# Regrouping the matmuls of a contraction step: pass by pass over the PSUM banks instead of chunk by chunk

## The chip, the core and the metric

The kernel runs on one NeuronCore of a Trainium2 chip. The metric is the device time of one execution in microseconds (us); for the kernel before it is 3276.52 us, the median of 3 runs.

## The reference, cut to what matters

One inference step of a two-layer decoder trunk of width 2048 over 1024 prompt positions and 8 x 8 sample positions, which makes 1088 token columns. All weights and activations are fp32.

```
layer 0:  z = rms_norm(h) @ w_in_a            # 2048 x 6144: a, b, gate
          c = a * sigmoid(b); y = silu(layer_norm(causal depthwise conv31(c)))
          h = h + rms_norm((y * silu(gate)) @ w_out_a)          # 2048 x 2048
layer 1:  k, v = rms_norm(h) @ w_kv           # 2048 x 512, 4 kv heads
          q, gate = rms_norm(h) @ w_in_b      # 2048 x 4096, 32 heads of 64
          o = sliding-window attention (128) with a sink per head
          h = h + rms_norm((o * silu(gate)) @ w_out_b)          # 2048 x 2048
```

Nearly all of the arithmetic is in the products with the weights, and they are what the change touches.

## The kernel before, in words

The data lie feature-major: 128 features on the partitions, 16 blocks of features (KT), 1088 tokens along the free axis. An output tile is 128 output features by all tokens. Its sum runs over 16 steps k, one for each block of input features. The products are made to near fp32 accuracy in three passes of a cheaper matmul type: activations and weights are each split into a rounded part (u_hi, w_hi) and the rest (u_lo, w_lo), and a tile sums u_hi\*w_hi, u_lo\*w_hi and u_hi\*w_lo.

The 1088 tokens are cut into three chunks of 364, 364 and 360 columns (CHUNKS). Each chunk of a tile has a PSUM bank of its own: z_even and z_odd are three banks each, and tiles alternate between the two. The PE function `tile(n, z, ...)` issues one tile. Its argument cs says which chunks take part: ALL (three chunks, 9 matmuls a step, 144 a tile), HEAD (the two chunks of 364 columns, 6 a step, 96 a tile) or TAIL (the chunk of 360 alone, 3 a step, 48 a tile). The program has 100 ALL tiles (32 for a and b of layer 0, called the GLU stage here, 16 for its gate, 16 for its output, 4 for k and v, 32 for q and the gate of layer 1), then 16 HEAD tiles and 16 TAIL tiles for the last output projection. Every matmul is preceded by a load of its 128x128 weights into the array, also when the weights are those of the matmul before it.

Inside a step the order before is: for each chunk the u_hi matmul (line 515) and then the u_lo matmul (line 516), both with w_hi and both into the same bank; after that, for each chunk, the w_lo matmul (line 518). So the w_lo pass already goes from bank to bank, while the other two passes write each bank twice in a row.

Around the matmuls, engines follow one another by semaphores, and each engine's order is written out by hand. The DMA queue of SP brings the weights in quarters of a tile (4 steps) to w_raw; ScalarE rounds them to w_hi (line 744) once PE has used the quarter of the tile before (w_used, raised by the last w_lo matmul of the quarter); GpSimd makes w_lo = w_raw - w_hi (line 1030) and raises w_lo_ready, for which PE waits ahead of each quarter. VectorE and ScalarE read a finished tile's three banks (z_read), and PE waits for that before it writes the same three banks two tiles later. In the GLU stage VectorE also computes the depthwise convolution (line 1327). In the q and gate tiles of layer 1 the attention matmuls are put between the steps of every second tile by the callback after_k.

Of the kernel before, what the change touches and what calls it, by code (L numbers as in the profile page):

```python
# [35 lines left out]
P = 128  # L36
# [6 lines left out]
CHUNKS = [(0, 364), (364, 364), (728, 360)]  # L43
# [46 lines left out]
def trunk_kernel(nc, x_t, state_t, ck_t, cv, w, cols_in, y_t, scp_t, ckp_t, cvp, scs_t, cks_t, cvs):  # L90
    ctx = ExitStack()
    with ctx:
        def sb(name, shape, dt=F32):
            return ctx.enter_context(nc.sbuf_tensor(name, shape, dt))
# [13 lines left out]
        u_hi = sb("u_hi", [P, KT, T], F32R)  # L108
        u_lo = sb("u_lo", [P, KT, T], F32R)
        w_raw = sb("w_raw", [P, NQ, 512])  # L110
        w_hi = sb("w_hi", [P, NQ, 512], F32R)
# [29 lines left out]
        cs = cs_flat.rearrange("p (b s) -> p b s", b=SB)  # L141
# [136 lines left out]
        def ge(eng, s, v):  # L278

            if not (isinstance(v, int) and v <= 0):  # L280
                eng.wait_ge(s, v)
# [4 lines left out]
        def chunk(ap, c):  # L286
            return ap[:, CHUNKS[c][0]:CHUNKS[c][0] + CHUNKS[c][1]]
# [213 lines left out]
        def _(pe):  # L501
            def tile(n, z, before_k=None, after_k=None, order=range(KT), cs=ALL):

                ge(pe, z_read, n - 1)
                seen = [0] * NQ
                for i, k in enumerate(order):
                    if before_k is not None:
                        before_k(i)
                    q, at = k // 4, P * (k % 4)
                    if seen[q] == 0:  # L510
                        pe.wait_ge(w_lo_ready, NQ * n + q + 1)
                    seen[q] += 1
                    for c in cs:
                        o = z[:, c, 0:CHUNKS[c][1]]
                        pe.matmul(o, w_hi[:, q, at:at + P], chunk(u_hi[:, k, :], c), start=(i == 0), stop=False)  # L515
                        pe.matmul(o, w_hi[:, q, at:at + P], chunk(u_lo[:, k, :], c), start=False, stop=False)  # L516
                    for c in cs:
                        mm = pe.matmul(z[:, c, 0:CHUNKS[c][1]], w_lo[:, q, at:at + P], chunk(u_hi[:, k, :], c),  # L518
                                       start=False, stop=(i == KT - 1))
                    if seen[q] == 4:  # L520
                        mm.then_inc(w_used, 1)
                    if after_k is not None:
                        after_k(i)
# [23 lines left out]

            pe.transpose(aux[:, 0, 0:SS], causal_ts[0:SS, :], ident[0:SS, 0:SS]).then_inc(mask_turned, 1)
            tile(0, z_even, lambda k: pe.wait_ge(u_lo_ready, k + 1))
            pe.wait_ge(sq_added, KT - 1)  # L550
            for c in range(3):
                mm = pe.matmul(z_odd[:, c, 0:CHUNKS[c][1]], ones[:, :], chunk(r_a, c), start=True, stop=True)
            mm.then_inc(sq_summed, 1)
            pe.wait_ge(var_ready, 1)
            tile(1, z_odd)
            with pe.Fori(1, KT) as i:
                tile(2 * i, z_even)
                tile(2 * i + 1, z_odd)
# [1045 lines left out]
```

## Time and profile before

| | us |
|---|---|
| median of 3 runs | 3276.52 (3274.56 to 3279.51) |
| the profiled execution | 3278.45 |
| its span | 3276.8 |
| PE busy in the span | 3075.6 (94%) |
| weight loads busy in the span | 2962.2 (90%) |
| VectorE, GpSimd, ScalarE busy | 1506.5, 1548.1, 850.2 |
| mean granted TensorE clock | 0.974 |
| matmuls, and weight loads | 19117 each |

The span is the profile's time from the first to the last instruction; the profiled execution's own time lies 1.65 us above it. A matmul's length in the records (0.33 us) is about twice the time from one start to the next, because matmuls are pipelined; what a matmul costs in a dense stretch is the distance of starts, and it is read from the timeline.

### The profile page before, as it was taken

The numbers are of one execution on the slowest core, as the hardware profiler recorded it, in microseconds if no ns is written. First come the engines' busy times: TensorE is split into PE (matmuls) and PEld (weight loads), VectorE is DVE, ScalarE is ACT, GpSimd is POOL, SyncE is SP. The second block draws the span as 40 slices with busy tenths as digits, with TensorE's granted clock in tenths as the row PEclk, the third lists the DMA queues.
The fourth block names the chain that finished last, engine by engine and source line by source line (L and its number), as shares of the span: only waits on it lengthen the run. The fifth ranks groups of instructions, "written<-read, shape, count | busy, mean of one in ns | idle before, by whom it ended". The sixth has DMA issues, their size and how long they took to land.

```text
span 3276.8 us, 50429 instructions
## 1 busy us (share of the span) xinstructions
PE 3075.6 (94%) x19117; PEld 2962.2 (90%) x19117; DVE 1506.5 (46%) x1729; ACT 850.2 (26%) x1708; POOL 1548.1 (47%) x1153
## 2 busy tenths in 40 slices
PE   6999999999989999999968999999999999899996
PEld 6999999999989999999947899899899889799985
DVE  6999999999931114000082233433443443500043
ACT  5121112211122214122142222322322322422332
POOL 2778778787733333333344233333333323244475
PEclk9999999999999999999989999999999999899998
DMA  5121221212122224222273211211211211432386
GB/s 163 41 71 50 57 60 47 71 50 57 51 92 95 89 96 170 71 65 72 86 253 113 64 48 43 61 45 45 58 42 48 61 39 48 157 95 87 108 290 219
DMA packets 171676, 284.86 MB, mean 87 GB/s; under 512 B 62008, under 2 KB 72504, under 8 KB 171576
## 3 DMA queue, kind: packets, MB, share of 16 engines
q1 hardware_dynamic: 127328, 222.48, 22.2%
q10 hardware_dynamic: 41912, 52.32, 4.4%
q0 software_dynamic: 2352, 8.88, 0.7%
q8 instruction: 60, 0.98, 0.1%
q14 instruction: 24, 0.20, 0.0%
HBM read 218.44 MB, written 67.15 MB: 87 GB/s over the span
## 4 chain that ended last, share of the span: by engine, by line
PE 46%; issue 23%; DVE 16%; ACT 5%; POOL 5%; DMA 3%; ACTq 1%; DVEq 1%; SPq 0%; POOLq 0%
PE z_even L515 8%; PE z_even L516 8%; PE z_even L518 8%; PE z_odd L515 7%; PE z_odd L516 6%; PE z_odd L518 6%; POOL w_lo L1030 3%; DVE aux L1327 3%; DVE work L1327 2%; DMA work<-conv_scratch 2%; ACT work L948 1%; DVE work L1423 1%; POOL work L1139 1%; DVE work L1426 1%; DVE work L1429 1%
## 5 line engine op out<-in xcount | busy, mean ns | idle before, releaser
L1030 POOL TENSOR_TENSOR w_lo<-w_raw,w_hi 128x512 fp32r<-128x512 f32 x528 | 745.2, 1420 | 1364.7 <-ACT w_hi L744 1364.2
L515 PE MATMUL z_even<-u_hi,w_hi 128*128 128x364 f32 (+1 forms) x2784 | 926.8, 333 | 88.9 <-POOL u_lo L1191 33.8
L515 PE MATMUL z_odd<-u_hi,w_hi 128*128 128x364 f32 (+1 forms) x2784 | 939.3, 337 | 58.0 <-POOL w_lo L1030 58.0
L516 PE MATMUL z_even<-u_lo,w_hi 128*128 128x364 f32 (+1 forms) x2784 | 923.0, 332 | 0.0
L516 PE MATMUL z_odd<-u_lo,w_hi 128*128 128x364 f32 (+1 forms) x2784 | 922.8, 331 | 0.0
L744 ACT ACTIVATE w_hi<-w_raw 128x512 fp32r<-128x512 f32 x528 | 331.3, 630 | 1681.7 <-PE z_even L518 804.6
L518 PE MATMUL z_odd<-u_hi,w_lo 128*128 128x364 f32 (+1 forms) x2784 | 636.6, 330 | 0.0
L518 PE MATMUL z_even<-u_hi,w_lo 128*128 128x364 f32 (+1 forms) x2784 | 635.9, 330 | 0.0
L515 PEld LDWEIGHTS z_even<-u_hi,w_hi 128*128 128x128 f32 x2784 | 531.0, 191 | 106.9 <-issue 35.8
L515 PEld LDWEIGHTS z_odd<-u_hi,w_hi 128*128 128x128 f32 x2784 | 531.6, 191 | 96.7 <-POOL w_lo L1030 54.5
L516 PEld LDWEIGHTS z_odd<-u_lo,w_hi 128*128 128x128 f32 x2784 | 532.2, 191 | 0.1
L516 PEld LDWEIGHTS z_even<-u_lo,w_hi 128*128 128x128 f32 x2784 | 531.7, 191 | 0.4 <-issue 0.3
L518 PEld LDWEIGHTS z_odd<-u_hi,w_lo 128*128 128x128 f32 x2784 | 488.4, 190 | 0.0
L518 PEld LDWEIGHTS z_even<-u_hi,w_lo 128*128 128x128 f32 x2784 | 487.7, 190 | 0.0
L1327 DVE SCALAR_TENSOR_TENSOR work<-work,cols 128x1024 f32<-128x1024 f32 x224 | 422.1, 1884 | 0.0
L1327 DVE SCALAR_TENSOR_TENSOR aux<-work,cols,aux 128x1024 f32<-128x1024 f32 x240 | 306.4, 1277 | 38.7 <-ACT aux L788 38.5
L1268 DVE TENSOR_SCALAR work<-z_even 128x364 f32<-128x364 f32 (+1 forms) x6 | 2.9, 530 | 657.4 <-PE z_even L543 657.4
L1278 DVE TENSOR_TENSOR work<-z_even,work 128x364 f32<-128x364 f32 (+1 forms) x126 | 59.4, 525 | 506.2 <-PE z_even L518 506.2
L1111 POOL TENSOR_TENSOR work<-work 128x480 f32<-128x480 f32 (+3 forms) x128 | 152.4, 1191 | 10.0
L1022 POOL TENSOR_TENSOR w_raw<-w_raw,cols 128x512 f32<-128x512 f32 x144 | 148.3, 1040 | 18.6 <-DMA branch_scratch<-work 18.6
L1103 POOL TENSOR_TENSOR work<-work,cols 128x248 f32<-128x248 f32 x128 | 130.2, 1048 | 2.9 <-POOL work L1115 2.9
L1139 POOL TENSOR_TENSOR work<-work 128x1088 f32<-128x1088 f32 x16 | 42.5, 2657 | 152.8 <-ACT work L809 140.1
(149 smaller groups left out, 2174.4 us busy)
## 6 DMA issues: line engine op xcount, KB each, us to landing
w_raw<-in_w SPq DMA_DIRECT2D x528, 256.0 KB, 2.6
work<-in_x SPq DMA_DIRECT2D x32, 544.0 KB, 5.3
work<-branch_scratch SPq DMA_DIRECT2D x31, 544.0 KB, 5.4
conv_scratch<-work ACTq DMA_DIRECT2D x16, 544.0 KB, 2.7
work<-conv_scratch SPq DMA_DIRECT2D x16, 544.0 KB, 3.8
resid_scratch<-work ACTq DMA_DIRECT2D x16, 544.0 KB, 5.6
branch_scratch<-work ACTq DMA_DIRECT2D x16, 512.0 KB, 2.6
branch_scratch<-work POOLq DMA_DIRECT2D x15, 544.0 KB, 3.0
```

The costliest lines, as they stand in the source:

```text
L515: pe.matmul(o, w_hi[:, q, at:at + P], chunk(u_hi[:, k, :], c), start=(i == 0), stop=False)
L516: pe.matmul(o, w_hi[:, q, at:at + P], chunk(u_lo[:, k, :], c), start=False, stop=False)
L518: mm = pe.matmul(z[:, c, 0:CHUNKS[c][1]], w_lo[:, q, at:at + P], chunk(u_hi[:, k, :], c), start=False, stop=(i == KT - 1))
L744: act.activation(w_hi[:, q, :], w_raw[:, q, :], ACT.Copy).then_inc(w_hi_ready, 1)
L948: ins = act.activation(sc[u][:, i, :], sc[u][:, i, :], ACT.Exp, scale=HD ** -0.5, bias=st[:, 4 + i:5 + i], accum_out=st[:, 16 + i:17 + i])
L1022: pool.tensor_tensor(w_raw[:, q, :].rearrange("p (k c) -> p k c", k=4), w_raw[:, q, :].rearrange("p (k c) -> p k c", k=4), cols[:, gain + ...
L1030: pool.tensor_tensor(w_lo[:, q, :], w_raw[:, q, :], w_hi[:, q, :].bitcast(F32), ALU.subtract).then_inc(w_lo_ready, 1)
L1103: ins = pool.tensor_tensor(pr[:, b], win, cols[:, bass.ds(C_CW + j * CW, CW)].unsqueeze(1).to_broadcast([P, SS, CW]), ALU.mult)
L1111: pool.tensor_tensor(pm[:, :, 0:m], pm[:, :, 0:m], pm[:, :, other:other + m], ALU.add).then_inc(pool_step, 1)
L1139: pool.tensor_tensor(s_st0, yb0[par], gg0[par], ALU.mult).then_inc(s_ready, 1)
L1278: ins = dve.tensor_tensor(chunk(out, c), z[:, c, 0:CHUNKS[c][1]], chunk(by, c), ALU.mult)
L1327: dve.scalar_tensor_tensor(out=acc, in0=cp[:, i:i + TP], scalar=cols[:, bass.ds(C_CW + j * CW + i, 1)], in1=acc, op0=ALU.mult, op1=ALU.add ...
```

## The change

In a step, the u_hi matmuls now go over all chunks first, then the u_lo matmuls go over all chunks, then the w_lo matmuls as before. No instruction is added or taken away, and the sum that each bank collects has the same terms. For a TAIL tile, with one chunk, the order is the one it had.

```diff
--- before.py
+++ after.py
@@ -511,9 +511,11 @@
                         pe.wait_ge(w_lo_ready, NQ * n + q + 1)
                     seen[q] += 1
                     for c in cs:
-                        o = z[:, c, 0:CHUNKS[c][1]]
-                        pe.matmul(o, w_hi[:, q, at:at + P], chunk(u_hi[:, k, :], c), start=(i == 0), stop=False)
-                        pe.matmul(o, w_hi[:, q, at:at + P], chunk(u_lo[:, k, :], c), start=False, stop=False)
+                        pe.matmul(z[:, c, 0:CHUNKS[c][1]], w_hi[:, q, at:at + P], chunk(u_hi[:, k, :], c),
+                                  start=(i == 0), stop=False)
+                    for c in cs:
+                        pe.matmul(z[:, c, 0:CHUNKS[c][1]], w_hi[:, q, at:at + P], chunk(u_lo[:, k, :], c),
+                                  start=False, stop=False)
                     for c in cs:
                         mm = pe.matmul(z[:, c, 0:CHUNKS[c][1]], w_lo[:, q, at:at + P], chunk(u_hi[:, k, :], c),
                                        start=False, stop=(i == KT - 1))
```

On PE, the second step of the first ALL tile (in a row: line, operation, target<-moving, stationary, size; "x2" two of them in a row), before:

```order
L515 MATMUL z_even<-u_hi,w_hi 128x364 [waits u_lo_ready]
L516 MATMUL z_even<-u_lo,w_hi 128x364
L515 MATMUL z_even<-u_hi,w_hi 128x364
L516 MATMUL z_even<-u_lo,w_hi 128x364
L515 MATMUL z_even<-u_hi,w_hi 128x360
L516 MATMUL z_even<-u_lo,w_hi 128x360
L518 MATMUL z_even<-u_hi,w_lo 128x364 x2
L518 MATMUL z_even<-u_hi,w_lo 128x360
```

and with the change:

```order
L514 MATMUL z_even<-u_hi,w_hi 128x364 [waits u_lo_ready]
L514 MATMUL z_even<-u_hi,w_hi 128x364
L514 MATMUL z_even<-u_hi,w_hi 128x360
L517 MATMUL z_even<-u_lo,w_hi 128x364 x2
L517 MATMUL z_even<-u_lo,w_hi 128x360
L520 MATMUL z_even<-u_hi,w_lo 128x364 x2
L520 MATMUL z_even<-u_hi,w_lo 128x360
```

The wait stays on the step's first matmul; the u_lo matmul of a chunk is no longer the one behind its u_hi matmul but three behind it, and no two consecutive matmuls write the same bank.

On PE, one step of a HEAD tile, before:

```order
L515 MATMUL z_even<-u_hi,w_hi 128x364
L516 MATMUL z_even<-u_lo,w_hi 128x364
L515 MATMUL z_even<-u_hi,w_hi 128x364
L516 MATMUL z_even<-u_lo,w_hi 128x364
L518 MATMUL z_even<-u_hi,w_lo 128x364 x2
```

and with the change:

```order
L514 MATMUL z_even<-u_hi,w_hi 128x364 x2
L517 MATMUL z_even<-u_lo,w_hi 128x364 x2
L520 MATMUL z_even<-u_hi,w_lo 128x364 x2
```

Here the two banks now take turns throughout the step. The rows of VectorE, ScalarE, GpSimd and SP, with their waits, are the same in both kernels but for line numbers.

## Rows read from the trace of the kernel before

**Rows 1.** Page, part 1: busy us (share of the span) xinstructions
```profile
PE 3075.6 (94%) x19117; PEld 2962.2 (90%) x19117; DVE 1506.5 (46%) x1729; ACT 850.2 (26%) x1708; POOL 1548.1 (47%) x1153
```

**Rows 2.** Busy time by engine: two stretches without a PE stall, and the GLU stage
```profile
core 0: us, PE busy (x) PEld busy (x) DVE busy (x) ACT busy (x) POOL busy (x), PEclk, DMA share, GB/s
1110.00:1252.00 142.00, 142.00 (x862) 142.00 (x861) 32.50 (x36) 33.87 (x41) 48.08 (x35) 1.00 0.33 113
2878.00:3098.00 220.00, 220.00 (x1340) 220.00 (x1339) 0.00 (x0) 58.72 (x112) 96.96 (x70) 1.00 0.29 90
...
80.00:1060.00 980.00, 934.62 (x5489) 925.47 (x5488) 812.60 (x654) 189.85 (x265) 692.58 (x501) 0.97 0.21 62
```

**Rows 3.** Waits of PE, the largest: engine line <- releaser: us in total, times, longest us
```profile
PE z_odd L515 <- POOL w_lo L1030: 58.0, 21, 5.1
```

**Rows 4.** Timeline of PE, two steps of a full tile: start us, length us, xcount
```profile
1117.36 0.33 PE L515 MATMUL z_even<-u_hi,w_hi 128*128 128x364 f32 x1
1117.53 0.33 PE L516 MATMUL z_even<-u_lo,w_hi 128*128 128x364 f32 x1
1117.69 0.33 PE L515 MATMUL z_even<-u_hi,w_hi 128*128 128x364 f32 x1
1117.86 0.33 PE L516 MATMUL z_even<-u_lo,w_hi 128*128 128x364 f32 x1
1118.02 0.33 PE L515 MATMUL z_even<-u_hi,w_hi 128*128 128x360 f32 x1
1118.19 0.33 PE L516 MATMUL z_even<-u_lo,w_hi 128*128 128x360 f32 x1
1118.36 0.66 PE L518 MATMUL z_even<-u_hi,w_lo 128*128 128x364 f32 x3
1118.85 0.33 PE L515 MATMUL z_even<-u_hi,w_hi 128*128 128x364 f32 x1
1119.01 0.33 PE L516 MATMUL z_even<-u_lo,w_hi 128*128 128x364 f32 x1
1119.18 0.33 PE L515 MATMUL z_even<-u_hi,w_hi 128*128 128x364 f32 x1
1119.34 0.33 PE L516 MATMUL z_even<-u_lo,w_hi 128*128 128x364 f32 x1
1119.51 0.33 PE L515 MATMUL z_even<-u_hi,w_hi 128*128 128x360 f32 x1
1119.67 0.33 PE L516 MATMUL z_even<-u_lo,w_hi 128*128 128x360 f32 x1
1119.84 0.66 PE L518 MATMUL z_even<-u_hi,w_lo 128*128 128x364 f32 x3
1120.34 0.33 PE L515 MATMUL z_even<-u_hi,w_hi 128*128 128x364 f32 x1
```

**Rows 5.** Timeline of PE, starts of two full tiles, 6 tiles (864 matmuls) apart
```profile
1109.93 0.33 PE L515 MATMUL z_even<-u_hi,w_hi 128*128 128x364 f32 x1
...
1252.65 0.33 PE L515 MATMUL z_even<-u_hi,w_hi 128*128 128x364 f32 x1
```

**Rows 6.** Timeline of PE, starts of a HEAD tile and the first TAIL tile, 1344 matmuls apart
```profile
2877.70 0.33 PE L515 MATMUL z_even<-u_hi,w_hi 128*128 128x364 f32 x1
...
3098.72 0.33 PE L515 MATMUL z_even<-u_hi,w_hi 128*128 128x360 f32 x1
```

**Rows 7.** Timeline of PE, first and last matmul of a TAIL tile, 47 apart
```profile
3125.01 0.33 PE L515 MATMUL z_odd<-u_hi,w_hi 128*128 128x360 f32 x1
...
3132.84 0.32 PE L518 MATMUL z_odd<-u_hi,w_lo 128*128 128x360 f32 x1
```

**Rows 8.** Timeline of PE behind a wait (in brackets), where the granted clock is 0.5
```profile
1274.89 0.64 PE L515 MATMUL z_even<-u_hi,w_hi 128*128 128x364 f32 x1 [4.25 <-POOL w_lo L1030]
...
1276.84 1.11 PE L518 MATMUL z_even<-u_hi,w_lo 128*128 128x364 f32 x3
1277.75 0.51 PE L515 MATMUL z_even<-u_hi,w_hi 128*128 128x364 f32 x1
```

## The prediction

> **What bounds the kernel now.** I read the page first, then the windows, then PE's waits and last its timeline. The page's first part has PE busy for 94% of the span with 19117 matmuls and as many weight loads; no other engine comes near [rows 1]. The windows show what that means in a stretch: between 1110 and 1252 us and between 2878 and 3098 us PE is busy for every microsecond at the full granted clock, 862 and 1340 matmuls in progress or started, while VectorE, ScalarE and GpSimd have slack [rows 2]. There the time is the number of matmuls times the distance between two starts. In the GLU stage (80 to 1060 us with the first gate tiles) PE is busy for 934.6 of 980 us and VectorE, with the convolution, for 812.6 [rows 2]: PE still sets the pace, but short waits lie between its tiles. The longest kind, for w_lo from GpSimd, sums to 58.0 us over the run in 21 waits of up to 5.1 us [rows 3]. So the only thing that this change can move is the distance of matmul starts, and wherever PE is dense it moves the end one for one.
>
> **The distance of starts, and whether the bank is in it.** Six ALL tiles, 864 matmuls, go from 1109.93 to 1252.65: 142.72 us, so 0.16519 us a matmul and 1.4867 us a step of nine [rows 5]. Fourteen HEAD tiles, 1344 matmuls, all of 364 columns, take 221.02 us: 0.16445 each [rows 6]. A TAIL tile, all of 360 columns, takes 7.83 us for 47 distances: 0.1666 each [rows 7]. These three stages differ in what the change is about. In TAIL every matmul writes the bank of the one before it. In ALL 3 of 9 do (u_lo behind u_hi of the same chunk), in HEAD 2 of 6. If the distance depended on the chunk alone, a step of ALL would be 6 x 0.16445 + 3 x 0.1666 = 1.4865 us. Measured is 1.4867. That leaves nothing for the bank.
>
> The timeline says the same within a step [rows 4]. In the two steps from 1117.36 the six distances from a u_hi to the u_lo matmul on the same bank are three of 0.17 and three of 0.16, 0.99 us together: 0.165 each. The six from a u_lo matmul to the next one, on another bank, sum to 1.00: 0.1667. The w_lo pass, which already goes from bank to bank, takes 0.49 and 0.50 us for its three, 0.165 each. Writing a bank twice in a row is not dearer than changing it.
>
> At the half clock it is the same [rows 8]: three w_lo matmuls on three banks, from 1276.84 to 1277.75, take 0.91 us, 0.303 each, which is 364 columns at 1.2 GHz and nothing besides. At full clock 364 columns would be 0.1517 us, and 0.16445 are taken. So there is an excess of 0.0128 us a matmul that could in principle be won, but rows with and without a change of bank show the same excess.
>
> **The change part by part.**
> - Removed, added: no instruction, no load of weights, no wait, no DMA. The six matmuls with w_hi in a step keep w_hi, so the array's weights change in value as often as before.
> - Moved: in 1600 steps of ALL (100 tiles x 16) and 256 of HEAD, the u_lo matmuls of chunks 0 and 1 go later by up to two places, and the u_hi matmuls of the later chunks go forward. 3 x 1600 + 2 x 256 = 5312 same-bank neighbours become other-bank neighbours. The 256 TAIL steps are untouched. Cost of a changed neighbour: bounds from the nearest rows are the smallest and the largest single distance of [rows 4], 0.16 and 0.17, against the mean 0.165. That is -0.005 to +0.005 each, or -27 to +27 us. I take 0, by the ALL step that comes out as the sum of its chunks [rows 5 to 7], since that is the same instruction mix over 864 matmuls and not one stamp rounded to 0.01.
> - Waits: the wait for w_lo_ready and that for u_lo_ready stand ahead of the step's first matmul in both. The last matmul of a quarter, which frees w_hi and w_lo for ScalarE and GpSimd, and the last three of a tile, which free the banks for VectorE and ScalarE, are the w_lo pass, unchanged. No other engine is told anything earlier or later: 0. This rests on PE's own pace; if that changed, a gain in the GLU stage would partly turn into more waiting behind the 58.0 us of [rows 3], while a loss would be paid whole.
> - Sum: span 3276.8 + 0, plus 1.65 us around it, is 3278.45 for the profiled execution; that stands 1.93 us above the median of the runs, so the median stays at **3276.5 us**.
>
> A rule that speaks for the change is in the Trainium skill, page "Perfetto Trace Analysis", section "Matmul Optimizations": see that all eight PSUM banks are used, for the most instruction-level parallelism. The kernel uses three banks in a step either way, and this case's rows show a pass over three banks no quicker than pairs on one. If the rule held for neighbours here, it would be the first rival below.
>
> **The rivals.**
> 1. *Back-to-back writes of one bank do cost something, and the excess is part of it.* For it: TAIL, all same-bank, has the largest distance although its matmuls are shorter. Taken as a bank effect: excess over columns at full clock is 0.1666 - 0.1500 = 0.0166 in TAIL and 0.0128 in HEAD, where a third are same-bank; the slope is 0.0038 / (2/3) = 0.0057 us a same-bank neighbour. 5312 x 0.0057 = 30 us less, 3246 us. Against it: the same slope gives an ALL step of 9 x (0.1511 + 0.0128) = 1.475 us and 1.4867 are measured, and the pairs of [rows 4] are not slower. If all of the excess of the 10624 matmuls of the first two passes went, it would be 136 us; nothing in the w_lo pass supports that.
> 2. *Slower: changing the bank is what costs.* [Rows 4] have 0.1667 for other-bank neighbours with w_hi against 0.165 for same-bank ones. If the new neighbours all take 0.1667, it is 0.0017 x 5312 = 9 us more, 3285.5 us, +0.27%. It decides if the u_hi and u_lo passes have three distances of over 0.166 each. Against it: the w_lo pass has 0.165, and the difference is a rounding of the stamps.
> 3. *The clock.* TensorE granted 1.00 in both dense stretches [rows 2]. At half clock a step of nine takes 6 x 0.303 + 3 x 0.300 = 2.72 us in place of 1.487 [rows 5, 8], so each microsecond at half clock costs 0.45. The half clock of [rows 8] stands behind a wait of 4.25 us, and none lies in the dense stretches. A mean of 0.974 means some 170 us at half; if rotating banks brought on as much again, it would be +77 us, 3353 us. The Trainium skill has such a rule, page "TensorE: Matmul & The Clock Gate", section "A second HAM failure mode: psum-queue depth-cycling": cycling through banks made small idles between groups and the clock swung. The trace speaks against it here: a third of the matmuls cycle already at clock 1.00.
> 4. *A shift of pace.* The distances within a step are uneven, 0.16 or 0.17, and repeat from step to step; how the reads of the moving columns fall together may differ in the new order, which now reads a row of u_hi from end to end. If one distance in a step goes from 0.165 to 0.16 or 0.17, that is 0.005 us over 1856 steps, 9 us either way: 3267 or 3286 us.
> 5. *The change isn't in effect.* The issued order shows it in ALL and HEAD and not in TAIL; that leaves the forecast's time anyway.
>
> **How the numbers follow.** About 0.2% (6.6 us) is what a measurement of this kernel can tell from no change. Chances: no effect of the order 0.70, with 3272 to 3281; rival 1 0.06; rival 2 0.09; rival 3 0.02; rival 4 0.08 faster, 0.04 slower; 0.01 for the rest. Faster by over 0.2%: 0.06 + 0.08 + 0.01 = 0.15. Slower: 0.09 + 0.02 + 0.04, of which some stays under the bound, 0.13. Same: 0.72. The range takes in rivals 2 and 4 and leaves out 1 and 3: 3265 to 3288 us.
>
> **What would show it.** Right: starts of two ALL tiles six apart again 142.7 us apart, HEAD 0.1644, TAIL 0.1666, granted clock 0.97, waits for w_lo within a few us of 58. Rival 1: ALL tiles of 24 rather than 23.8 us become 23.5 us, TAIL unchanged. Rival 2: 23.9 us. Rival 3: a mean clock well below 0.97, with half-clock stretches where PE doesn't wait. Rival 4: a uniform shift of ALL tiles by about 0.1 us with another pattern of 0.16 and 0.17. Wrong altogether: ALL unchanged and the time moved, which would mean that another engine's timing hangs on the order.

## The result, and the profile after

| | us |
|---|---|
| median of 5 runs, changed kernel | 3293.58 (3291.88 to 3295.39) |
| median of 5 runs, kernel before | 3279.06 (3274.56 to 3279.51) |
| ratio of the times | 1.0046, 95% interval 1.0034 to 1.0057 |
| profiled execution, and its span | 3291.88, 3290.2 (before 3278.45, 3276.8) |
| mean granted TensorE clock | 0.977 (before 0.974) |

The kernel became slower by 14.5 us between the medians (0.44%; 0.46% by the ratio of the times), where no change was forecast and 3288 us was the upper end of the range. The page's first part has the same instructions and more time in them, 3092.1 us of PE against 3075.6 [rows 1]:

```profile
PE 3092.1 (94%) x19117; PEld 2978.7 (91%) x19117; DVE 1506.2 (46%) x1729; ACT 850.6 (26%) x1708; POOL 1556.3 (47%) x1153
```

The timeline of PE shows a step of an ALL tile of the changed kernel and the start of the next (start us, length us). The three passes now stand as three rows of three matmuls (lines 514, 517 and 520 are the u_hi, the u_lo and the w_lo matmul):

```profile
1134.80 0.66 PE L514 MATMUL z_odd<-u_hi,w_hi 128*128 128x364 f32 x3
1135.30 0.66 PE L517 MATMUL z_odd<-u_lo,w_hi 128*128 128x364 f32 x3
1135.80 0.66 PE L520 MATMUL z_odd<-u_hi,w_lo 128*128 128x364 f32 x3
1136.30 0.66 PE L514 MATMUL z_odd<-u_hi,w_hi 128*128 128x364 f32 x3
```

Each pass takes 0.50 us, 0.1667 a matmul, and the steps around it are the same. Before, a step had 0.49 or 0.50 for its w_lo pass and 0.99 to 1.00 for the six others [rows 4]. So the w_lo pass became slower too, though the change leaves it as it was: averaged over undisturbed tiles of the output stage, its three distances were 0.159, 0.168 and 0.168 us and are now 0.165, 0.167 and 0.168, which is nearly half of what a step lost. Over long stretches the timeline's starts give the pace exactly: two ALL tiles six apart, then the first whole HEAD tile and the first TAIL tile, fourteen apart:

```profile
1110.80 0.49 PE L514 MATMUL z_even<-u_hi,w_hi 128*128 128x364 f32 x2
...
1254.80 0.49 PE L514 MATMUL z_even<-u_hi,w_hi 128*128 128x364 f32 x2
...
2892.04 0.50 PE L514 MATMUL z_even<-u_hi,w_hi 128*128 128x364 f32 x2
...
3116.04 0.33 PE L514 MATMUL z_even<-u_hi,w_hi 128*128 128x360 f32 x1
```

ALL: 144.00 us for 864 matmuls where it was 142.72 [rows 5]. HEAD: 224.00 us for 1344 where it was 221.02 [rows 6]. An ALL step is 1.5000 us in place of 1.4867, a HEAD step 1.0000 in place of 0.9867. Both steps lost the same 0.0133 us, though one has nine matmuls and the other six. These paces hold in every stage: of the ALL tiles that no wait, half clock or other work of PE interrupts, all 58 have 1.487 us a step before and all 59 have 1.500 after.

The windows say where in the run it went. After, GLU stage from its third tile, gate, output of layer 0, k/v and q with the gate of layer 1, HEAD, TAIL:

```profile
core 0: us, PE busy (x) PEld busy (x) DVE busy (x) ACT busy (x) POOL busy (x), PEclk, DMA share, GB/s
83.17:843.47 760.30, 733.23 (x4321) 729.59 (x4321) 716.71 (x567) 142.96 (x206) 600.67 (x433) 0.98 0.21 57
843.47:1254.80 411.33, 396.54 (x2318) 391.34 (x2318) 135.31 (x134) 90.91 (x112) 162.92 (x115) 0.98 0.29 93
1254.80:1668.06 413.26, 390.76 (x2318) 388.44 (x2317) 36.14 (x23) 98.86 (x179) 138.20 (x88) 0.98 0.25 82
1668.06:2842.29 1174.23, 1113.80 (x7554) 1024.47 (x7554) 476.68 (x895) 333.69 (x926) 406.95 (x320) 0.98 0.23 69
2842.29:3116.04 273.75, 263.72 (x1537) 260.26 (x1537) 17.82 (x14) 80.68 (x139) 112.72 (x82) 0.98 0.37 113
3116.04:3290.20 174.16, 135.59 (x781) 131.43 (x780) 72.98 (x59) 56.28 (x100) 112.50 (x86) 0.92 0.76 255
```

The same six stretches before:

```profile
82.84:845.38 762.54, 731.86 (x4321) 727.92 (x4321) 719.03 (x567) 142.87 (x206) 596.13 (x433) 0.98 0.21 56
845.38:1252.65 407.27, 392.57 (x2318) 387.36 (x2317) 134.74 (x134) 91.16 (x112) 161.70 (x115) 0.97 0.28 94
1252.65:1661.46 408.81, 386.98 (x2317) 384.66 (x2317) 36.69 (x24) 98.51 (x179) 139.04 (x89) 0.98 0.25 83
1661.46:2830.55 1169.09, 1106.87 (x7554) 1017.80 (x7554) 476.50 (x895) 333.79 (x926) 404.32 (x320) 0.98 0.22 69
2830.55:3098.72 268.17, 261.48 (x1537) 257.93 (x1537) 17.80 (x14) 80.57 (x139) 112.95 (x82) 0.97 0.36 116
3098.72:3276.80 178.08, 137.81 (x781) 133.62 (x780) 71.24 (x59) 56.30 (x100) 111.64 (x86) 0.91 0.75 250
```

From the first column to the next: GLU 762.54 to 760.30 (-2.2), gate +4.1, output +4.5, k/v and q +5.1, HEAD +5.6, TAIL -3.9. With +0.3 ahead of the third tile that is the 13.4 us of the span. At 0.0133 us a step the pace alone asks for 3.4, 3.4, 7.7 and 3.4 us in the four stages between GLU and TAIL: 17.9, against 19.2 measured, the rest being waits between tiles that vary from run to run. In GLU it asks for 480 x 0.0133 = 6.4 us and none of it appears. PE's largest group of waits, over the whole run, shrank from 58.0 us [rows 3] to 51.3:

```profile
PE z_odd L514 <- POOL w_lo L1032: 51.3, 20, 4.7
```

The TAIL stage has the same order of instructions in both kernels; in the runs below that leave it so it lasts 175.7 to 178.9 us by the same windows. Most of its -3.9 us is such a spread, and no run ties it to the change.

### The profile page after: what moved, and what is told of

Same layout as the page of the kernel before. It is cut to its first block, busy times and chain, and to the rows that moved or that the text cites. A ratio compares the mean times of both kernels' runs of the same rounds, so it can differ in the third digit from the quotient of the medians.

```text
span 3290.2 us, 50429 instructions
## 1 busy us (share of the span) xinstructions
PE 3092.1 (94%) x19117; PEld 2978.7 (91%) x19117; DVE 1506.2 (46%) x1729; ACT 850.6 (26%) x1708; POOL 1556.3 (47%) x1153
## 4 chain that ended last, share of the span: by engine, by line
PE 46%; issue 23%; DVE 17%; ACT 5%; POOL 5%; DMA 3%; ACTq 1%; DVEq 1%; SPq 0%; POOLq 0%
PE z_even L514 8%; PE z_even L517 8%; PE z_even L520 8%; PE z_odd L514 7%; PE z_odd L517 6%; PE z_odd L520 6%; POOL w_lo L1032 3%; DVE aux L1329 3%; DVE work L1329 2%; DMA work<-conv_scratch 2%; ACT work L950 1%; DVE work L1425 1%; DVE work L1428 1%; POOL work L1141 1%; DVE work L1431 1%
## 5 line engine op out<-in xcount | busy, mean ns | idle before, releaser
L514 PE MATMUL z_even<-u_hi,w_hi 128*128 128x364 f32 (+1 forms) x2784 | 649.6, 335 | 92.9 <-POOL u_lo L1193 33.2
L514 PE MATMUL z_odd<-u_hi,w_hi 128*128 128x364 f32 (+1 forms) x2784 | 659.0, 338 | 51.3 <-POOL w_lo L1032 51.3
L517 PE MATMUL z_even<-u_lo,w_hi 128*128 128x364 f32 (+1 forms) x2784 | 642.9, 332 | 0.0
L517 PE MATMUL z_odd<-u_lo,w_hi 128*128 128x364 f32 (+1 forms) x2784 | 641.3, 332 | 0.0
L514 PEld LDWEIGHTS z_even<-u_hi,w_hi 128*128 128x128 f32 x2784 | 490.7, 191 | 111.8 <-issue 36.3
L514 PEld LDWEIGHTS z_odd<-u_hi,w_hi 128*128 128x128 f32 x2784 | 483.4, 190 | 89.4 <-POOL w_lo L1032 47.4
L517 PEld LDWEIGHTS z_even<-u_lo,w_hi 128*128 128x128 f32 x2784 | 493.3, 191 | 0.0
L517 PEld LDWEIGHTS z_odd<-u_lo,w_hi 128*128 128x128 f32 x2784 | 492.1, 190 | 0.1
```

The costliest lines, as they stand in the source:

```text
L514: pe.matmul(z[:, c, 0:CHUNKS[c][1]], w_hi[:, q, at:at + P], chunk(u_hi[:, k, :], c), start=(i == 0), stop=False)
L517: pe.matmul(z[:, c, 0:CHUNKS[c][1]], w_hi[:, q, at:at + P], chunk(u_lo[:, k, :], c), start=False, stop=False)
```

## The experiments

The ALL step of each run is read as before from the starts of two tiles six apart in the gate stage, the HEAD step from starts fourteen tiles apart; both are at full granted clock without a wait. The label of each run stands in brackets. In most orders the other stages have the same ALL pace, and where they don't, this is said. Numbers 1 to 6 and alternating_no_repeat were timed once each: that gives the pace, but a difference of a few us in the run's time says nothing, since the kernel before alone spreads over 3277.2 to 3284.4 us on one chip.

**1. Operands as before, banks as in the changed kernel** (pairs_rotating_banks).

```diff
-for c in cs:
-    o = z[:, c, 0:CHUNKS[c][1]]
-    pe.matmul(o, w_hi[:, q, at:at + P], chunk(u_hi[:, k, :], c), start=(i == 0), stop=False)
-    pe.matmul(o, w_hi[:, q, at:at + P], chunk(u_lo[:, k, :], c), start=False, stop=False)
+seen_banks = set()
+for lo, c, to in [(j % 2, cs[j // 2], cs[j % len(cs)]) for j in range(2 * len(cs))]:
+    u = u_lo if lo else u_hi
+    pe.matmul(z[:, to, 0:CHUNKS[c][1]], w_hi[:, q, at:at + P], chunk(u[:, k, :], c),
+              start=(i == 0 and to not in seen_banks), stop=False)
+    seen_banks.add(to)
```

> The operand order of the kernel before (u_hi, u_lo of chunk 0, then of chunk 1, of chunk 2), but the six matmuls write banks 0,1,2,0,1,2 as in the changed kernel; HEAD 0,1,0,1. Sums land in the wrong bank, so what is computed is not the products any more; matmuls, loads and waits are the same in number and size. Theory BANK (a matmul on another bank than its neighbour is what costs): an ALL step takes 1.500 us, ALL tile 24.0 us, HEAD step 1.000, run about 3291 us. Theory OPERAND (the order in which u_hi and u_lo are read is what costs, banks do not matter): ALL step 1.487, HEAD step 0.987, run about 3278 us.

The timeline of this run, starts of two ALL tiles six apart:

```profile
1110.21 0.33 PE L516 MATMUL z_even<-u_hi,w_hi 128*128 128x364 f32 x1
...
1252.93 0.33 PE L516 MATMUL z_even<-u_hi,w_hi 128*128 128x364 f32 x1
```

142.72 us, the kernel before to the hundredth; HEAD 221.01 us for fourteen tiles. The run took 3277.72 us, the kernel before on the same chip 3282.81. No matmul of a step writes its neighbour's bank, and it costs nothing.

**2. Operands as in the changed kernel, banks as before** (passes_paired_banks). It is the same table with another rule from the second step on (cut; the first step of a tile keeps the order of before, with 364 columns for chunk 2):

```diff
-for lo, c, to in [(j % 2, cs[j // 2], cs[j % len(cs)]) for j in range(2 * len(cs))]:
+for lo, c, to in [(j // len(cs), cs[j % len(cs)], cs[j // 2]) for j in range(2 * len(cs))]:
```

> The operand order of the changed kernel (u_hi of chunks 0,1,2, then u_lo of 0,1,2), but the six matmuls write banks 0,0,1,1,2,2 as the kernel before does; HEAD 0,0,1,1. The first of the 16 steps of a tile keeps the order of before, with 364 columns for chunk 2. Sums land in the wrong bank, so what is computed is not the products. Theory BANK: ALL step 1.487 us, HEAD 0.987, run about 3278 us. Theory OPERAND: ALL step 1.500, HEAD 1.000, run about 3291 us.

```profile
1112.04 0.33 PE L521 MATMUL z_even<-u_hi,w_hi 128*128 128x364 f32 x1
...
1256.00 0.33 PE L521 MATMUL z_even<-u_hi,w_hi 128*128 128x364 f32 x1
```

143.96 us for six tiles, of whose 16 steps one has the old order: if 15 steps are of 1.500, one is of 1.493. HEAD took 223.81 us for fourteen tiles. The run took 3295.62 us. Theory BANK is out from both sides: the banks of before with the operands of after are slow, the reverse is quick. The order in which the moving columns are read does it.

**3. Fewer and more columns** (columns_300, columns_400). All three passes take their bank and their columns from this function; columns_400 has 400 in all steps of ALL tiles in place of the first line.

```diff
+def part(c):
+    n = 300 if len(cs) == 3 and i else CHUNKS[c][1]
+    at0 = min(CHUNKS[c][0], T - n)
+    return z[:, c, 0:n], slice(at0, at0 + n)
```

> The kernel before, but in ALL tiles every matmul from the second step on reads and writes only 300 columns (64 or 60 columns of each chunk get only the first step's terms). Theory STREAM (a distance of starts is the columns at 2.4 GHz plus about 0.013 us for anything that follows): 0.125 + 0.013 = 0.138 us a matmul, 1.24 us a step, tiles of 20 us, the run limited by other engines in the GLU stage. Theory LOAD (something that does not depend on the columns, such as the load of weights between two matmuls, sets the distance at about 0.165 us): distance stays 0.160 to 0.167 us, step 1.44 to 1.50, run within 1% of 3278 us.

> The kernel before, but in ALL tiles every matmul reads and writes 400 columns (the extra ones land in columns of the bank that nobody reads; chunk 2 reads columns 688 to 1087 and its tokens are shifted). Theory STREAM: 0.1667 + 0.013 = 0.180 us a matmul, 1.62 us a step, run about 3500 us. Theory LOAD: the larger of 0.165 and the 0.1667 us that 400 columns take at 2.4 GHz, so 0.167 to 0.170, 1.50 to 1.53 a step, run 3290 to 3340 us.

Starts of two ALL tiles six apart, with 300 columns:

```profile
1079.01 0.33 PE L521 MATMUL z_even<-u_hi,w_hi 128*128 128x364 f32 x1
...
1199.53 0.33 PE L521 MATMUL z_even<-u_hi,w_hi 128*128 128x364 f32 x1
```

and with 400:

```profile
1140.48 0.34 PE L521 MATMUL z_even<-u_hi,w_hi 128*128 128x400 f32 x1
...
1296.64 0.34 PE L521 MATMUL z_even<-u_hi,w_hi 128*128 128x400 f32 x1
```

With 300: 120.52 / 6 less one step of 1.487 leaves 18.600 for fifteen, 1.240 us a step, 0.1378 a matmul. With 400: 0.1807 a matmul (in the output stage 0.1815, 1.633 a step where the gate stage has 1.627). Above the columns at 2.4 GHz (0.1250, 0.1667) that is 0.0128 and 0.0140; the kernel before has 0.1652 - 0.1511 = 0.0141. The runs took 3076.16 and 3419.01 us. So the distance is the stream of columns and an excess of about 0.013 to 0.014 us behind each; LOAD falls. It is this excess that the order moves, to 0.1667 - 0.1511 = 0.0156 in the changed kernel.

The windows of the same two runs over the GLU stage (span, PE, PEld, DVE, ACT, POOL), 300 columns first:

```profile
81.09:837.15 756.06, 634.79 (x4322) 631.12 (x4321) 715.45 (x566) 142.37 (x206) 598.97 (x433) 0.91 0.21 57
```

```profile
86.40:867.20 780.80, 780.80 (x4322) 780.80 (x4321) 701.75 (x570) 143.57 (x207) 575.26 (x433) 1.00 0.20 55
```

With matmuls a sixth shorter the stage still lasts 756.06 us, 6.5 less than before, and VectorE is busy for 95% of it; with 400 columns PE is busy throughout and the stage lasts 780.80. So some 756 us are set there by something other than PE's pace. Rows of the waits in the stage with 300 columns (us in total, times, longest us):

```profile
POOL w_lo L1035 <- ACT w_hi L749: 144.2, 23, 10.0
...
PE z_odd L521 <- POOL w_lo L1035: 121.3, 15, 9.8
ACT work L777 <- DVE aux L1338: 113.9, 14, 9.3
```

PE waits for w_lo from GpSimd. Part of that begins at VectorE: ScalarE waited 7.98 us for it, made w_hi only behind that work, at 436.21 us, and GpSimd's w_lo followed at 436.92. Part is GpSimd's own: its w_lo of 415.24 us stood behind 16 us of its other work, and PE had waited 6.76 us for it. ScalarE's waits for the DMA of w_raw (143.8 us) lead back to GpSimd as well, for whose w_lo SP waits 255.2 us before it issues them. VectorE is the engine that is busy for nearly all of the stage, but no run here changes its work or GpSimd's, so which of them sets the floor stays open. Before, at 762.54 us, the stage lay close to that floor, and a small change of PE's pace is taken up by PE's waits: over the fourteen kernels here whose passes stream 1088 columns, both of the comparison among them, the stage lasts 760.0 to 766.6 us, whether an ALL step takes 1.480 or 1.500.

**4. Chunk starts at multiples of 16 columns** (chunks_368_pairs, chunks_368_passes): CHUNKS = [(0, 368), (368, 368), (736, 352)], in both orders.

> The order of the kernel before, with chunks of 368, 368 and 352 columns, so that every chunk begins at a multiple of 16 columns (64 bytes of a row); HEAD covers 736 tokens, TAIL 352. Theory ALIGN (the 0.013 us that the order moves come from where the chunks begin, 364 and 728 columns into a row not being multiples of 16): ALL step differs from 1.487 us, and the step is the same here in both orders. Theory SWITCH (reading u_hi and u_lo in turn is cheaper than reading on in the same row, wherever chunks begin): this order stays about 0.013 us a step below the other one, ALL step near 1.487 since the columns are 1088 in all either way.

> The order of the changed kernel, with chunks of 368, 368 and 352 columns. Theory ALIGN: ALL step equal to that of the run with these chunks in the order of before. Theory SWITCH: ALL step 1.500 us, 0.013 above it.

ALL steps: 1.480 us in pairs, 1.490 in passes, read from 142.08 and 143.04 us for six tiles. HEAD, now with 736 columns in place of 728: 1.0067 and 1.015. The run in pairs took 3279.18 us, in passes 3292.23, the kernel before on that chip 3282.98. ALIGN falls as the cause, for the order still moves the step by 0.010 when all chunks begin at such multiples; but the cut has an effect of its own, 0.007 to 0.010 us less an ALL step in either order. It isn't shown that the starts do it, since the lengths changed with them. In HEAD it goes the other way: beyond the columns at 2.4 GHz (0.920 us for a step of 3 x 736, 0.910 for 3 x 728) a step has 0.087 us in pairs and 0.095 in passes, where the cut of before has 0.077 and 0.090.

**5. Other orders with the same computation** (chunk_by_chunk, the first line, and pairs_then_w_reversed, the second).

```diff
+for what, c in [(w, c) for c in cs for w in "HLW"]:
+for what, c in [(w, c) for c in cs for w in "HL"] + [("W", c) for c in cs[::-1]]:
```

> All three passes of a chunk in a row: u_hi, u_lo with w_hi, then u_hi with w_lo, then the next chunk; computes the same. Changes between u_hi and u_lo in a step: 6, as before (the changed kernel has 2). The weights' value changes 6 times a step in place of 2. Theory SWITCH: step 1.487 us or less, HEAD 0.987 or less. If it is the w_lo pass in order that carries the saving: 1.500. If changing the weights' value costs: above 1.500.

> The kernel before with the w_lo pass over the chunks in descending order (2, 1, 0); computes the same. In the kernel before the pass's first distance is the short one (0.159 us) in ALL steps. Theory SWITCH: it is still 1.487 us, as the u_hi/u_lo pairs are unchanged. Theory FOLLOW (a matmul that reads on where the last one ended has another distance than one that jumps within the row): the step changes, since the pass no longer reads a row from start to end.

chunk_by_chunk has two paces. In the gate stage six ALL tiles took 144.00 us, 1.500 a step; in the output stage, with the same instructions in the same order, they took 142.71, the 1.487 of before:

```profile
1110.59 0.33 PE L514 MATMUL z_even<-u_hi,w_hi 128*128 128x364 f32 x1
...
1254.59 0.33 PE L514 MATMUL z_even<-u_hi,w_hi 128*128 128x364 f32 x1
...
1333.53 0.33 PE L514 MATMUL z_odd<-u_hi,w_hi 128*128 128x364 f32 x1
...
1476.24 0.33 PE L514 MATMUL z_odd<-u_hi,w_hi 128*128 128x364 f32 x1
```

Between the two lies a wait of 4.64 us for w_lo. Both paces occur in the GLU stage too, where most of the changes from one to the other lie behind a wait. Nothing here shows what picks one of them. HEAD took 222.51 us, 0.993 a step, where SWITCH asked for 0.987 or less. pairs_then_w_reversed: 143.68 us, 1.497, in all stages, and HEAD 0.993. Runs of 3287.66 and 3287.67 us on the chip of number 4. SWITCH falls by pairs_then_w_reversed, which changes tensors as often as before and is slower in every stage; of chunk_by_chunk's ALL tiles only those at 1.500 speak against it. Turning one pass around costs three quarters of what the whole change does.

**6. The same places without another tensor** (u_hi_twice): the second matmul of a pair reads u_hi again.

> The kernel before, with the second matmul of each pair reading u_hi again in place of u_lo (the term of u_lo is left out, that of u_hi counted twice). The columns' places in the row come in the same sequence, chunks 0 0 1 1 2 2 0 1 2, and no matmul changes the tensor it reads. Theory REPEAT (a matmul that reads the same chunk's place as the one before it starts a little sooner): ALL step 1.487 us, HEAD 0.987. Theory SWITCH (the saving comes with changing between u_hi and u_lo): 1.500 and 1.000.

```profile
1110.55 0.33 PE L515 MATMUL z_even<-u_hi,w_hi 128*128 128x364 f32 x1
...
1253.27 0.33 PE L515 MATMUL z_even<-u_hi,w_hi 128*128 128x364 f32 x1
```

142.72 us again, and HEAD 221.01; the run took 3282.21 us. Which of the two tensors is read is of no account. What is left is the sequence of chunk places: 0 0 1 1 2 2 0 1 2 before, 0 1 2 0 1 2 0 1 2 after.

**7. Is it the repeated place?** (alternating_no_repeat, w_in_pairs). The first (the upper line) takes places 0 2 1 0 2 1 0 1 2, the second adds repeats by taking the w_lo matmuls of two steps together.

```diff
+seq = [("H", 0), ("L", 2), ("H", 1), ("L", 0), ("H", 2), ("L", 1)]
+if i % 2:
+    for c in cs:
+        for kk in (order[i - 1], k):
+            mm = pe.matmul(z[:, c, 0:CHUNKS[c][1]], w_lo[:, kk // 4, P * (kk % 4):P * (kk % 4) + P],
+                           chunk(u_hi[:, kk, :], c), start=False, stop=(i == KT - 1 and kk == k))
```

> In ALL steps u_hi 0, u_lo 2, u_hi 1, u_lo 0, u_hi 2, u_lo 1, then the w_lo pass 0 1 2; computes the same. HEAD and TAIL as before. Six changes of tensor a step, as in the kernel before, and no chunk twice in a row. Theory REPEAT: the saving is gone, ALL step 1.497 us or more. Theory SWITCH: 1.487 us or less.

> The kernel before with the w_lo matmuls of two steps taken together: for each chunk that of step k and that of step k+1, so that this pass too reads each chunk's place twice in a row; computes the same. Neighbours on one chunk go from 3 a step to 4.5. Theory REPEAT, if savings add: 0.0067 us a repeat pair of chunks 0 and 1, so 1.480 us a step, a run 10 us below before (3272 us). Theory SWITCH: no gain, 1.487 to 1.493 a step. The last w_lo matmul of a quarter stays its last matmul, so the weights come free no later.

alternating_no_repeat, starts six ALL tiles apart:

```profile
1112.59 0.33 PE L519 MATMUL z_even<-u_hi,w_hi 128*128 128x364 f32 x1
...
1254.67 0.33 PE L519 MATMUL z_even<-u_hi,w_hi 128*128 128x364 f32 x1
```

142.08 us, 1.480 a step: quicker than before without any repeat, so REPEAT falls as the rule; the run took 3279.77 us. w_in_pairs had 142.08 in the gate stage, as its theory asks, but tiles of 23.84 us (1.490 a step) in the output stage with the very same instructions, and HEAD steps of 0.995. So it is another order with two paces, both of which occur in its GLU stage. Its run took 3284.62 us where 3272 was asked for, 1.0013 times before (1.0004 to 1.0022): a miss, and a sign that the pace is not a sum of fixed prices.

**8. The direction** (passes_descending, pairs_descending): in the changed kernel and in the one before, every `for c in cs` of a step becomes `for c in cs[::-1]`.

> The changed kernel with every pass over the chunks in the order 2, 1, 0; computes the same. Theory NEIGHBOURS (a distance depends on the places in the row of the matmul and of the one before; a step is the sum over its neighbours): from the runs so far one ascending round 0-1-2-0 is 0.500 us, and the step of alternating_no_repeat (1.480 = two descending rounds and one ascending) gives a descending round of 0.490. So an ALL step of three descending rounds is 1.470 us, HEAD (0-1-0-1 either way) stays 1.000, and the run comes out some 25 to 30 us below the changed kernel outside the GLU stage, about 3266 to 3275. Theory GROUPING (passes of distinct chunks are dear, pairs cheap): 1.500 as in the changed kernel, run 3293.

> The kernel before with chunks in the order 2, 1, 0 in the pairs and in the w_lo pass; computes the same. Theory NEIGHBOURS: repeats of a place 0.4867 us for the three, two descending rounds of 0.490: 1.4667 us an ALL step, 0.020 below before; HEAD 0.987 as before. Outside the GLU stage 68 ALL tiles x 16 x 0.020 = 22 us less, run about 3256 us if no new waits come, and no more than 3270. Theory GROUPING: 1.487 as before, run 3279.

The timeline of passes_descending, first and last row of the ALL stretch of six tiles, then the HEAD stretch:

```profile
1109.00 0.49 PE L514 MATMUL z_even<-u_hi,w_hi 128*128 128x360 f32 x2
...
1251.08 0.49 PE L514 MATMUL z_even<-u_hi,w_hi 128*128 128x360 f32 x2
...
2874.05 0.50 PE L514 MATMUL z_even<-u_hi,w_hi 128*128 128x364 f32 x2
...
3098.05 0.33 PE L514 MATMUL z_even<-u_hi,w_hi 128*128 128x360 f32 x1
```

Six tiles take 142.08 us: 1.480 a step, 0.020 below the changed kernel with the same grouping into passes. HEAD, where 2-1-0 becomes 1-0, stays at 224.00. The run: 3276.99 us, above the 3266 to 3275 expected, 0.9988 of before (0.9979 to 0.9997). GROUPING falls: in passes, the direction is worth 0.020 us a step, more than the 0.013 between passes and pairs. But NEIGHBOURS is right in sign only: it asked for 1.470. pairs_descending contradicts it outright: 143.36 us, 1.493 a step where 1.467 was asked for, HEAD 0.993 where 0.987 was, and a run of 3286.65 us, 1.0017 times before (1.0008 to 1.0026). Turning the pairs around costs, turning the passes around gains.

**9. The quicker order of each stage** (descending_all_pairs_head): ALL tiles as in passes_descending, HEAD and TAIL as in the kernel before.

> ALL tiles pass by pass over the chunks 2, 1, 0 (step 1.480 us in passes_descending), HEAD and TAIL tiles in the order of the kernel before (HEAD step 0.987); computes the same. If the paces of the stages add: HEAD 3.4 us below passes_descending, ALL as there, so 7 us (0.2%) below the kernel before on the same chip. If the waits between tiles take it back: within 4 us of before.

3272.99 us against 3281.00 on the same chip, 0.9976 (0.9964 to 0.9987): 8.0 us where 7 were expected, and quicker than the kernel before; the changed kernel was not run beside it. Six ALL tiles take 142.08 us, the HEAD stretch 221.01. Its gate stage lasts 407.59 us, its output stage 406.54 and k/v with q 1166.44. Against before these are +0.3, -2.3 and -2.7 us, where the pace alone asks for -1.7, -1.7 and -3.8; the rest are waits between tiles, which differ from run to run.

## Why the prediction was wrong, point by point

- *The bank is not in the distance.* Right. Numbers 1 and 2 show it by swapping banks and operands apart. Rival 1 falls with it. The rows behind it were weaker than they looked. HEAD and ALL have the same share of same-bank neighbours, a third, so that only the TAIL term spoke of banks, and its 0.1666 came from one tile. Other TAIL tiles of the same trace run quicker with the same instructions, at full granted clock; in this one 47 distances take 7.69 us, 0.1636 each:

```profile
3171.12 0.33 PE L515 MATMUL z_even<-u_hi,w_hi 128*128 128x360 f32 x1
...
3178.81 0.32 PE L518 MATMUL z_even<-u_hi,w_lo 128*128 128x360 f32 x1
```

- As to the rule of the Trainium skill, page "Perfetto Trace Analysis", section "Matmul Optimizations", on using all eight banks: number 1 shows no gain from taking three in turn within a step (142.72 us either way), and no run here uses eight.
- *"I take 0, by the ALL step that comes out as the sum of its chunks."* This is the step that failed. The term put at nothing, the cost of a changed neighbour, measured 0.0133 us a step. The sum 6 x 0.16445 + 3 x 0.1666 = 1.4865 does agree with 1.4867, but by luck, twice over. In the changed kernel all nine matmuls of an ALL step and all six of a HEAD step average 0.1667. Before, each step, of nine or of six matmuls, was 0.0133 us short of that: 1.5000 - 0.0133 and 1.0000 - 0.0133. HEAD's mean of 0.16445 had the saving of its own order in it, and the sum built from it closed because the two savings happen to be equal. And with the 0.1636 of the TAIL tile above it would have been 1.4775. What the sum could speak of was banks; it was then used for the order in which columns are read, of which it says nothing, since ALL and HEAD have that order in common.
- *The bounds, -27 to +27 us.* A step went up by 0.0133 us. Put down to the changed neighbours alone, that is 0.0044 for each of the three of an ALL step, and 0.0067 for each of the two of a HEAD step, the latter above the 0.005 allowed for; but the w_lo pass, which has none, took nearly half of it in ALL. Over 1856 steps it is 24.7 us, inside the bounds; 14.5 appeared.
- *Rival 2, slower, +9 us, 9%.* Right in direction, and its reading of [rows 4] (0.1667 behind a u_lo matmul) was, by luck, the average that came. Its reason, the bank, was wrong. In the sum it was mis-sized, since all nine distances of a step average 0.1667 and not six.
- *Rival 4, the rhythm of the reads, 12% in all.* This is the nearest to what happened: the distances changed with the order of the reads, "which now reads a row of u_hi from end to end". Its price of 0.005 us a step was too small by 0.008, and its sign was left open.
- *"A loss would be paid whole."* Wrong in the GLU stage: 6.4 us were due, and the stage got 2.2 shorter. [Rows 2] had VectorE at 812.6 of 980 us, read as slack. Number 3 shows a floor of about 756 us that PE's pace doesn't set.
- *The clock.* No fall: 0.977 against 0.974. The rule of the Trainium skill, page "TensorE: Matmul & The Clock Gate", section "A second HAM failure mode: psum-queue depth-cycling", does not show in this trace: the dense stretches cycle through three banks at a granted clock of 1.00.
- *What would show it.* The signs named for rival 4 came, a uniform shift of ALL tiles (by 0.21 us, from 23.79 to 24.00) with another pattern within the step. The line for rival 1 gave 24 us as the length of the tiles before, by mistake; it was 23.79.

What stays open: why the excess behind a matmul depends on the sequence of places. A price for each pair of neighbouring places can't be the answer: the w_lo pass has the same neighbours before and after, with other distances, and chunk_by_chunk and w_in_pairs hold one order at two paces. So an order allows one or more steady paces, and nothing here shows what decides between them. The kernel before and the changed one kept one ALL pace each, in 58 and 59 undisturbed tiles of all stages, so that the loss between them doesn't hang on this. The cut of the columns takes part (number 4). No run here looked at the reads themselves.

## What to carry to other kernels

In a stream of matmuls that is bound by PE, the order in which a row's pieces are read was worth up to 1.3% of the pace here, apart from banks and tensors; try a few orders that compute the same, descending among them, and read the distance of starts over some hundred matmuls. Read it in more than one stage: one stage of chunk_by_chunk or of w_in_pairs alone would have given the wrong pace for the rest. A sum that closes is evidence only for what differs between its parts. And a stage's busiest engine is not its only bound: here, with a second one busy for 94%, PE's waits for the others absorbed a small gain or loss of its own pace.

## What was not expected of the hardware

- At full clock an ALL step of nine matmuls over the same 3264 columns took 1.480, 1.487, 1.490, 1.493, 1.497 or 1.500 us, by the order and the cut of the columns, and in two of the orders by the stage; at half clock three matmuls took 0.91 us, with no excess at all [rows 8].
- In the changed kernel, steps with matmuls of 360 columns (ALL) and without (HEAD) both average 0.1667 us a matmul, which at 2.4 GHz is 400 columns.
- The same instructions can run at two paces: w_in_pairs had 23.68 us a tile in one stage and 23.84 in another, chunk_by_chunk 24.00 and 23.79, and TAIL tiles of the kernel before 0.1666 or 0.1636 a matmul.
